# Delta-rule rows split into f16 halves first and turned into columns by a DMA, not by TensorE

## The reference

```
v_new = u_i - w_i @ S
o     = qd_i @ S + qk_i @ v_new
S     = S * exp(gl_i) + kd_i.T @ v_new
...
o = rmsnorm(o, out_norm) * silu(z)
```

## Time and profile before

| | us |
|---|---|
| median of 3 runs | 3220.5 (3218.71 to 3221.18) |
| the profiled execution | 3224.77 |
| its span | 3223.2 |
| PE busy | 2965.6 (92%) |
| DVE busy | 2581.3 (80%) |
| ACT busy | 1972.9 (61%) |
| POOL busy | 945.3 (29%) |

### The profile page before, as it was taken

One profiled execution on the slowest core, in us unless ns is written; L12 is line 12 of the kernel. 1 busy time (PEld: TensorE's weight loads), 2 busy tenths in 40 slices (PEclk: granted clock), 3 DMA queues, 4 the chain that ended last, 5 costly groups with the idle time before them and its releaser, 6 DMA issues. The chain is left out here.

```text
span 3223.2 us, 81340 instructions
## 1 busy us (share of the span) xinstructions
PE 2965.6 (92%) x28442; PEld 2210.3 (69%) x28443; DVE 2581.3 (80%) x7135; ACT 1972.9 (61%) x4385; POOL 945.3 (29%) x994
## 2 busy tenths in 40 slices
PE   5888999999999999999999999996799999999960
PEld 4777788878888887888788878874344455554530
DVE  5788788888888888888788888886788788888845
ACT  6455565556556565656565655653677677777746
POOL 4323122222212221312222122212344344444420
PEclk8889999999999999999999999998899999999985
DMA  6110332222222222222222222225487777777749
GB/s 229 51 49 14 80 93 80 74 80 73 74 81 75 78 74 86 67 77 71 87 67 80 75 79 74 74 73 209 118 268 226 234 196 209 194 219 215 227 99 394
DMA packets 186113, 396.52 MB, mean 123 GB/s; under 512 B 86992, under 2 KB 86992, under 8 KB 173520
## 3 DMA queue, kind: packets, MB, share of 16 engines
q1 hardware_dynamic: 148896, 286.22, 26.2%
q0 software_dynamic: 29216, 89.30, 12.1%
q10 hardware_dynamic: 7696, 16.86, 1.3%
HBM read 280.05 MB, written 96.01 MB: 117 GB/s over the span
## 5 line engine op out<-in xcount | busy, mean ns | idle before, releaser
L618 PE MATMUL pj<-uT,W 128*128 128x128 f16 x15744 | 980.4, 220 | 10.8 <-POOL W L1925 10.8
L618 PEld LDWEIGHTS pj<-uT,W 128*128 128x128 f16 x15744 | 934.5, 99 | 58.0 <-issue 47.8
L2283 DVE SCALAR_TENSOR_TENSOR W<-W,ecol 128x512 f16<-128x512 f16 x664 | 447.6, 747 | 107.9 <-ACT W L2227 105.1
L2227 ACT ACTIVATE W<-W,ecol 128x512 f16 x664 | 415.9, 708 | 79.5 <-issue 77.1
L2191 PE MATMUL bA<-W,uT 128*128 128x512 f16 x1992 | 448.1, 382 | 5.7 <-issue 4.4
L2191 PEld LDWEIGHTS bA<-W,uT 128*128 128x128 f16 x1992 | 193.9, 98 | 230.0 <-issue 12.1
L2175 PE MATMUL pj<-W,qs 128*128 x664 | 302.3, 598 | 1.4 <-ACT qs L2254 0.9
L1986 POOL TENSOR_TENSOR dec<-tri,g 128x512 f32<-128x512 f32 x33 | 34.3, 1039 | 860.3 <-DVE g L1715 860.3
L1017 ACT ACTIVATE ht<-ht 128x512 f32<-128x512 f32 x256 | 159.2, 623 | 95.3 <-DMA ht<-w_up 89.6
L2175 PEld LDWEIGHTS pj<-W,qs 128*128 128x128 f32 x664 | 120.8, 192 | 123.0 <-issue 122.7
L1047 ACT ACTIVATE qh<-bA 128x256 f32<-128x256 f32 x198 | 76.6, 387 | 190.4 <-PE bA L784 186.5
(11 more groups left out here) (506 smaller groups left out, 6214.7 us busy)
## 6 DMA issues: line engine op xcount, KB each, us to landing
ht<-w_gate SPq DMA_DIRECT2D x128, 256.0 KB, 3.1
ht<-w_up SPq DMA_DIRECT2D x128, 256.0 KB, 3.3
W<-w_gate SPq DMA_DIRECT2D x32, 1024.0 KB
W<-w_up SPq DMA_DIRECT2D x32, 1024.0 KB
W<-w_down SPq DMA_DIRECT2D x32, 1024.0 KB
x_in<-xm SPq DMA_DIRECT2D x33, 512.0 KB, 4.2
ht<-xm SPq DMA_DIRECT2D x32, 512.0 KB, 4.0
h_rows<-ht SPq DMA_DIRECT2D x32, 512.0 KB
```

The source lines that it names most:

```text
L618: mm = pe.matmul(pj[g % 2][:, j, :], w16[:, k, w_half(w_high, COL[GROUPS[g]], 512, j * P, P)], (ul if low_u else uh)[:, k, :], start=(k == ...
L2227: nc.scalar.activation(part_of(wx[par][:, 0], k), raw[:, k], ACT.Copy, scale=ecol[par][:, k:k + 1]).then_inc(sem("wx_high"), 1)
L2283: a = nc.vector.scalar_tensor_tensor(out=part_of(wx[par][:, 1], k), in0=raw[:, k], scalar=ecol[par][:, k:k + 1], in1=part_of(wx[par][:, 0] ...
```

## The change

`yt` is split as rows. ACT's high half moves ahead of `x_stats` and reads `yt` in SBUF; DVE's low half moves from behind level 4 to behind the logits, ahead of two taps of the first convolution. Both write f16 rows into `ks`, which is free then (`yd_rows`). SyncE then issues one transposing DMA from there to `yd16`, over `yt`, between the `u_rows` store and the wait for it. PE's four transposes go; `w_out_part(s, 4)` waits for the DMA, and DVE waits for it ahead of the convolution that writes `ks`. PE's waits for `yd_ready` ahead of `rank` and of the turning of `X` go, the latter's in favour of `kd_ready`. In the drain `low_delta` keeps its place, ahead of the second norm.

```diff
--- before.py
+++ after.py
@@ -273,6 +273,7 @@
 
         yl16 = yl[:].rearrange("p j n -> p (j n)").bitcast(F16).rearrange("p (s j n) -> p s j n", s=2, j=4)
         yd16 = yt[:].rearrange("p j n -> p (j n)").bitcast(F16).rearrange("p (s j n) -> p s j n", s=2, j=4)
+        yd_rows = ks[:].rearrange("p j n -> p (j n)").bitcast(F16)
         gw = yl[:].rearrange("p j n -> p (j n)")[:, 0:KT * (NG + NE)].rearrange("p (k n) -> p k n", k=KT)
         lgx = sb("lgx", [P, 3, NG + NE])
         ht = sb("ht", [P, D])
@@ -531,6 +532,9 @@
                             sp.wait_ge(sem("idx_zeroed"), ZEROED)
                         sp.dma_start(u_rows[bass.ds(s.pR * P, P), :], ht[:]).then_inc(sem("u_stored"), 16)
                     if s.O:
+                        need(sp, sem("yd_ready"), s.nO)
+                        sp.dma_start(yd16.rearrange("p s j n -> p (s j) n"), yd_rows, transpose=True).then_inc(sem("yd_full"), 16)
+                    if s.O:
                         need(sp, sem("u_stored"), 16 * s.nR)
                     raw_chunks(s)
                     if len(s.sums) < 2:
@@ -665,7 +669,7 @@
                             need(pe, sem("z_done"), s.nP)
                             need(pe, sem("lg_raw"), s.nR)
                         if j == 4:
-                            need(pe, sem("yd_ready"), s.nO)
+                            need(pe, sem("yd_full"), 16 * s.nO)
                         for jr in ((), (), (1, 0, 2), (3,), (4,), (5,), (6,), (7,))[j]:
                             for part, w_high in ((0, False), (0, True), (1, True)):
                                 y = yl16[:, part, jr, :] if jr < 4 else yd16[:, part, jr - 4, :]
@@ -686,17 +690,8 @@
                         return
                     need(pe, sem("oh_ready"), s.nR)
                     need(pe, sem("T7_new"), s.nG)
-                    need(pe, sem("yd_ready"), s.nO)
                     pe.matmul(bTf[:, 0:NE], tri16[:], ohs[:], start=True, stop=True)
                     pe.matmul(bTf[:, NE:2 * NE], ones16[:], ohs[:], start=True, stop=True).then_inc(sem("rank_full"), 1)
-
-                def turn_delta(s):
-
-                    need(pe, sem("yt_ready"), s.nO)
-                    need(pe, sem("kd_ready"), s.nG)
-                    for h in range(H):
-                        mm = pe.transpose(bT[:, h, :], yt[:, h, :], ident[:])
-                    mm.then_inc(sem("yd_full"), 1)
 
                 def late_part(s, *parts):
 
@@ -872,8 +867,6 @@
                     level_y(s, 3)
                     project(s, 2, 1)
                     level_x(s, 3)
-                    if s.O and s.G:
-                        turn_delta(s)
                     project(s, 2, 2)
                     level_y(s, 4)
                     project(s, 2, 3)
@@ -903,11 +896,10 @@
                     if s.O and not s.G:
                         pe.wait_ge(sem("fro_act"), 2)
                         pe.matmul(bA[:, 0, 0:NE], ones[:], fsum[:], start=True, stop=True).then_inc(sem("fro_full"), 1)
-                        turn_delta(s)
                     late_part(s, 2)
                     if s.G:
                         need(pe, sem("X_new"), 6 * s.pG + 5)
-                        need(pe, sem("yd_ready"), s.nO)
+                        need(pe, sem("kd_ready"), s.nG)
                         for h in range(H):
                             mm = pe.transpose(bT[:, (h + 2) % H, :], X[:, h, :], ident[:])
                         mm.then_inc(sem("T7_full"), 1)
@@ -1188,6 +1180,9 @@
                         nc.scalar.activation(hh, hh, ACT.Ln, bias=tiny[:]).then_inc(sem("ib_step"), 1)
                         need(act, sem("ib_step"), 2 * s.pG + 1)
                         nc.scalar.activation(hh, hh, ACT.Exp, scale=0.5).then_inc(sem("ib_step"), 1)
+                    if s.O:
+                        need(act, sem("yt_ready"), s.nO)
+                        nc.scalar.activation(yd_rows[:, 0:512], flat(yt), ACT.Copy).then_inc(sem("yd_high"), 1)
                     x_stats(s)
                     level_y(s, 2)
                     x_norm(s)
@@ -1197,9 +1192,6 @@
                     level_y(s, 3)
                     if s.G:
                         raw_squares(s, twice=(0,))
-                    if s.O:
-                        need(act, sem("yd_full"), s.nO)
-                        nc.scalar.activation(yd16[:, 0], bT[:], ACT.Copy).then_inc(sem("yd_high"), 1)
                     level_y(s, 4)
                     if s.G:
                         raw_squares(s, twice=(1,))
@@ -1550,7 +1542,7 @@
                 def low_delta(s):
 
                     need(dve, sem("yd_high"), s.nO)
-                    nc.vector.tensor_tensor(yd16[:, 1], bT[:], yd16[:, 0], ALU.subtract).then_inc(sem("yd_ready"), 1)
+                    nc.vector.tensor_tensor(yd_rows[:, 512:1024], flat(yt), yd_rows[:, 0:512], ALU.subtract).then_inc(sem("yd_ready"), 1)
 
                 def low_lru(s):
 
@@ -1796,6 +1788,8 @@
                     if s.R and s.G:
                         second_norm(s)
                         logits(s)
+                    if s.O and s.G:
+                        low_delta(s)
                     conv(s, 0, xc, 2, 3)
                     level_x(s, 3)
                     if s.G:
@@ -1811,14 +1805,14 @@
                     if s.O and s.G:
                         lru_rows(s)
                     level_x(s, 4)
-                    if s.O and s.G:
-                        low_delta(s)
                     conv(s, 1, qs, 1)
                     if s.O and s.G:
                         low_lru(s)
                     level_x(s, 5)
                     conv(s, 1, qs, 2, 3)
                     level_x(s, 6)
+                    if s.P:
+                        need(dve, sem("yd_full"), 16 * s.nO)
                     conv(s, 2, ks, 0, 1, 2, 3)
                     level_x(s, 7)
                     if s.R and s.G:
```

## The result

Over 20 executions each the changed kernel takes 3230.51 us (3220.9 to 3235.16), the kernel before 3219.62 (3211.15 to 3230.29): a ratio of 1.0033, 95% interval 1.0024 to 1.0041, some 11 us slower. The forecast was 3235.5, slower.

A forecast was written before the change was run, and what follows sets the result against it. The prediction took a path through PE, DVE, ACT and back to PE at level 5 as the bound; 9.9 us in steps plus 5 in the drain, +15, carried to the 3220.5 median gave 3235.5 us, range 3229 to 3242.

The forecast's parts named there:

- The bound: In a step, the critical path runs PE level 3, DVE, ACT, PE level 5; the removed transposes lie beside it.
- PE's meeting with DVE's `T`: Ahead of level 5, PE's earlier waits for DVE take up only part of the 0.43 us PE gained.
- The moved low half: On DVE ahead of level 3: 0.60 us less slack lengthens each step 0.33 us, +9.9 us over 30 steps.
- Slack: On DVE at level 3: L1496 could have started 0.27 us earlier than it did.
- ACT's high half: On ACT ahead of `x_stats`: a 0.63 us copy, covered by 1.48 us idle ahead of level 2, worth 0.
- PE's transposes: Ahead of level 5: removing 0.43 us of PE work only lengthens PE's wait there, worth 0.
- PE's dropped waits: On PE: the removed waits had long been met, worth 0.
- the DMA: On SyncE's queue: issue 1.24 us, landing 3.2 us, with 2.6 us of cover for the raw pieces, worth 0.
- The drain: In step 33 nothing hides the DMA, so PE waits for columns: +5 us once (3.4 to 7); step 32 costs 0.
- PE as the bound: Rival: PE sets the step and its 0.43 us count, giving 3212.6 us; chance 0.12.
- The low half hidden: Rival: DVE hides the moved low half, steps stay unchanged and only the drain is paid, 3225.5 us; chance 0.16.
- The raw pieces held up: Rival: the transposing DMA delays raw pieces on SyncE's queue, 0.6 us a step, 3253 us; chance 0.08.

The follow-up runs named there:

- e8: Kernel before with ACT's second raw square moved behind its copy for level 5: 3224.14 us, ratio 1.0011, step 63.40 us.
- e11: Changed kernel, low half behind level 4, DMA behind two raw pieces, PE's transposes in steps 2, 4, 32, 33, ACT's raw square and DVE's level 6 moved: 3199.3 us.
- e10: Kernel before with ACT's second raw square behind its level 5 copy and DVE's level 6 ahead of the queries' convolution's last tap: 3207.32 us, ratio 0.9959.
- e2: Changed kernel with four transposes of the identity put back on PE at the old place: 3229.73 us, ratio 1.0037 to the kernel before.
- e1: Kernel before with three of the four transposes left out in steps with a delta rule: 3221.62 us, ratio 1.0008.
- e12: Kernel before with only DVE's level 6 moved ahead of the queries' convolution's last tap: one execution, 3210.03 us against 3225.68; step 63.34 us.
- e3: Changed kernel with the low half computed twice in its new place: 3247.2 us, ratio 1.0097 to the kernel before.
- e4: Changed kernel with the low half back behind level 4 and the DMA behind two raw pieces: 3239.13 us, ratio 1.0064 to the kernel before.
- e5: Changed kernel with only the transposing DMA moved behind the first two raw pieces: 3238.18 us, ratio 1.0055 to the kernel before.

## Why the prediction was right

- **The bound.** Right, and shown: PE's 98.7% hid a path through DVE and ACT. Transposes out of the one kernel and back into the other leave the steps at 63.40 and 63.67 us. One detail was off: PE's meeting with DVE's `T` was to take up only part of the 0.43 us that PE gained. It took all of it, 0.48 us ahead of level 4, and PE then came to level 5 0.08 us later in the step than before. For the step this changes nothing, since ACT's `qh` ends the wait there.
- **The moved low half.** Forecast 0.33 us a step, measured 0.28. The term itself held: 0.32 us later from PE's level 3 to PE's level 5. Some 0.04 us came back behind level 5, where I had every engine keep its distance; there the path of level 6 had been late by a few hundredths, which e8 laid bare. I had not looked at it. Summed over steps 2 to 31 the profiles differ by 7.5 us, not 9.9: 1.5 of the 2.4 are this, and 1.0 is a single step of the kernel before that took 64.69 us.
- **Slack.** Right to 0.02 us: 0.61 us of instruction less 0.32 that came through is 0.29, forecast 0.27. Low half twice: +0.60 us a step, the whole instruction.
- **ACT's high half, PE's transposes, PE's dropped waits, the DMA: 0.** Right. The DMA lands in 3.4 us (forecast 3.2), and issuing took 1.31 us in a usual step (forecast 1.24), up to 2.40 in a few. Its cover of 2.6 us was never used up: at worst the first raw piece left 2.2 us later after the store than before. The Trainium skill's 1309 ns for one 128x128 block ("VectorE: DVE Perf Modes", "The three transpose paths"), taken eight times, does not describe this transfer: eight blocks land in 3.4 us. The Trainium skill's advice on the same page, under "Rules for kernel authors", to use TensorE where the result may lie in PSUM was not borne out by e11 either, where the step with the DMA is 0.24 us shorter than e10's.
- **The drain.** Forecast +5, measured +5.5 in the profile, but by another split, so that the sum fits in part by luck. The 5 us were worked out for step 33 alone, which gives 3.6: PE waits 3.58 us for the columns (forecast 4.7), and six products at half clock add 1.2 (forecast 1.6). The other 1.9 us come in step 32, which I had put at 0. There PE's granted clock is longer at its lower level. These are the first 42 us of step 32, first in the kernel before and the changed one, then in e2 and e8; the third number from the end is the mean granted clock:

```profile
2181.70:2223.70 42.00, 30.68 (x182) 21.76 (x182) 26.49 (x69) 12.03 (x27) 12.38 (x11) 0.84 0.56 225
2186.68:2228.68 42.00, 30.57 (x165) 21.75 (x165) 24.99 (x61) 11.95 (x27) 12.38 (x11) 0.76 0.57 222
```

```profile
2186.91:2228.91 42.00, 31.25 (x167) 22.36 (x167) 24.97 (x61) 11.96 (x27) 12.38 (x11) 0.76 0.56 220
2178.40:2220.40 42.00, 31.17 (x166) 22.36 (x166) 24.97 (x61) 12.04 (x27) 12.40 (x11) 0.76 0.54 217
```

  The missing transposes are not the reason: e2 has them back and shows 0.76 as well, e1 has three of them out and shows 0.84. Nor is it the change as a whole: e8, the kernel before but for one raw square, has 0.76 too. PE's first product of step 33 starts 50.1 us after step 32's start in the kernel before and 52.1 in the changed one; it is 50.0 to 50.5 us in the three profiles with 0.84 (before, e1, e12) and 51.4 to 52.2 in the eleven others. What decides between the two stays open; the 1.9 us are not shown to be a cost of the change.
- **The sum.** 15 forecast, 11 measured (8 to 13 by the interval). The profiles' own count is 7.5 for steps 2 to 31 and 5.5 for the drain, 13.0. Beyond that the stages before and after vary by more than the rest of the difference from one profile to the next. The forecast's own low edge adds up to 10.9 us (0.25 x 30 + 3.4), that is 3231.4 and not 3229; the measured difference lies just there.
- **The rivals.** PE as the bound: excluded by e1 and e2. The low half hidden: excluded by e3, and by e4 with e5. The raw pieces held up: excluded for the steps by e5.

## What to carry to other kernels

An engine busy 98% of a stage is not yet its bound: look for the one place in the period where it still waits, follow that wait back, and ask on which side of the fork the removed and the added instructions lie. Where two paths are equally long, undoing one shows nothing; a change that looked worthless alone (either move here, or the DMA) pays when both are out of the way. What a long step hides must be looked at again in the first and last steps, where the cover is missing.

## What was unexpected of the hardware

DVE slows beside GpSimd in places where neither waits for the other by a semaphore. In the kernel before, one instruction of the queries' convolution (L1331, two inputs in SBUF) takes 344 ns at the median and 1432 ns at most, over 384 of them:

```profile
L1331 DVE SCALAR_TENSOR_TENSOR qs<-ext_q,cvw,qs x384: 311/344/1432, 161.2 to 2153.6; 128x128 f32<-128x128 f32 x192
```

Of the 384, 223 overlap no GpSimd instruction, and they take 311 to 352 ns; all 102 that take over 400 ns overlap one. The longest is about one GpSimd instruction (1.04 to 1.30 us) plus its own time. The Trainium skill has this in "SBUF — State Buffer", "Who interferes with whom": a VectorE instruction with two SBUF inputs contends with a GpSimd instruction that reads SBUF, and the port pair that the two share is an exclusive lock. The trace agrees, by the counts just given. It matters here because moving DVE's work earlier gained nothing: it ran into GpSimd's.
